# Expert stage of an encoder block on one core: eight pairs in a pipeline, rows gathered slot by slot, 16 KB weight rows, eleven weight halves loaded ahead

## What is computed

```python
def expert_choice_swiglu(h, w_router, w_gate, w_up, w_down):
    cap = EC_CAPACITY_FACTOR * seq // N_EXPERTS          # 64 slots per expert
    aff = softmax(einsum('bsd,de->bse', h, w_router))
    g, idx = lax.top_k(jnp.swapaxes(aff, 1, 2), cap)     # per expert, over tokens
    xin = h[idx]
    a = jnp.einsum('becd,edf->becf', xin, w_gate)
    u = jnp.einsum('becd,edf->becf', xin, w_up)
    y = jnp.einsum('becf,efd->becd', jax.nn.silu(a) * u, w_down) * g[..., None]
    return zeros.at[idx].add(y)                          # scatter-add of the rows

x = x + expert_choice_swiglu(rms_norm(x, norm2_g), ...)
return rms_norm(x, normf_g)
```

## Time and profile before

| | us |
|---|---|
| median of 3 runs | 959.29 (955.30 to 961.52) |
| the profiled execution, its own time | 957.11 |
| its span in the profile | 955.3 |
| PE busy | 884.0 (93%) |
| DVE, ACT, POOL busy | 340.6, 253.8, 22.8 |
| DMA | 239.66 MB, 251 GB/s over the span |

### The profile page before, as it was taken

The page is one execution under the profiler, slowest core; times in us unless marked ns, Lnnn a source line. Parts: engine busy times, 40 slices in busy tenths (PEclk is TensorE's granted clock), DMA queues, the critical chain, the costliest instruction groups (busy, mean ns, idle before and its releaser), DMA issues.

```text
span 955.3 us, 12190 instructions
## 1 busy us (share of the span) xinstructions
PE 884.0 (93%) x4932; PEld 573.9 (60%) x4932; DVE 340.6 (36%) x579; ACT 253.8 (27%) x488; POOL 22.8 (2%) x41
## 2 busy tenths in 40 slices
PE   4999899799989999997899988999899999899995
PEld 4999666577868888997635335353353533544432
DVE  4468767756625344337110032100230102301025
ACT  4433767665633323131111010110100100101102
POOL 1040000000000000000000000000000000000002
PEclk8999999999999999997999999999989999899997
DMA  8433111302137442916399999999999999999953
GB/s 258 94 90 89 45 45 45 110 17 83 39 112 241 138 121 61 372 53 264 133 378 409 410 409 384 381 409 410 408 410 405 410 410 409 410 409 410 410 236 110
DMA packets 115754, 239.66 MB, mean 251 GB/s; under 512 B 8960, under 2 KB 64384, under 8 KB 115456
## 3 DMA queue, kind: packets, MB, share of 16 engines
q1 hardware_dynamic: 110416, 235.95, 65.6%
q10 hardware_dynamic: 5296, 3.13, 1.2%
HBM read 236.96 MB, written 2.10 MB: 250 GB/s over the span
## 4 chain that ended last, share of the span: by engine, by line
PE 86%; DVE 7%; ACT 3%; issue 2%; DMA 1%; POOL 1%; SPq 0%; DVEq 0%; POOLq 0%; ACTq 0%
PE psum L1155 23%; PE psum L1186 12%; PE psum L819 10%; PE psum L821 10%; PE psum L820 10%; PE psum L1126 7%; PE psum L1203 3%; PE psum L956 2%; DVE x L1586 2%; PE psum L968 2%; DMA w_raw<-in_w_in 1%; PE psum L942 1%; PE psum L926 1%; PE psum L1169 1%; PE psum L978 1%
## 5 line engine op out<-in xcount | busy, mean ns | idle before, releaser
L1155 PE MATMUL psum<-wslot,xinT 128*64 128x512 f32 x1024 | 222.4, 593 | 4.9 <-ACT xinT L755 4.9
L1155 PEld LDWEIGHTS psum<-wslot,xinT 128*64 128x64 f32 x1024 | 72.5, 137 | 145.6 <-issue 139.3
L1186 PE MATMUL psum<-wslot,actT 128*64 128x512 f32 x512 | 111.6, 594 | 5.7 <-ACT actT L770 5.7
L1279 DVE TENSOR_TENSOR w_lo<-w_raw,w_hi 128x1024 fp32r<-128x1024 f32 (+1 forms) x56 | 65.2, 1185 | 77.3 <-ACT w_hi L543 77.0
L819 PE MATMUL psum<-hT_hi,w_hi 128*128 128x512 f32 x224 | 88.9, 397 | 1.4 <-DVE qB_next L1377 1.4
L821 PE MATMUL psum<-hT_hi,w_lo 128*128 128x512 f32 x224 | 87.5, 390 | 0.0
L820 PE MATMUL psum<-hT_lo,w_hi 128*128 128x512 f32 x224 | 87.4, 390 | 0.0
L1566 DVE TENSOR_TENSOR act<-act,psum 128x512 f32<-128x512 f32 x16 | 11.0, 688 | 210.5 <-ACT act L766 210.5
L1186 PEld LDWEIGHTS psum<-wslot,actT 128*64 128x64 f32 x512 | 36.5, 137 | 75.7 <-issue 71.1
L1126 PEld LDWEIGHTS psum<-pick,xn 128*128 128x128 f32 x512 | 62.8, 205 | 13.3 <-issue 6.5
L1126 PE MATMUL psum<-pick,xn 128*128 128x128 f32 x512 | 65.1, 290 | 5.4 <-DVE pick L1559 5.4
(11 more groups left out here) (169 smaller groups left out, 1181.0 us busy)
## 6 DMA issues: line engine op xcount, KB each, us to landing
wslot<-in_w_gate SPq DMA_DIRECT2D x64, 1024.0 KB, 14.1
wslot<-in_w_up SPq DMA_DIRECT2D x64, 1024.0 KB, 16.9
wslot<-in_w_down SPq DMA_DIRECT2D x64, 1024.0 KB, 10.8
w_raw<-in_w_in SPq DMA_DIRECT2D x40, 512.0 KB, 4.5
w_raw<-in_w_out SPq DMA_DIRECT2D x8, 512.0 KB, 7.5
x_in<-in_x SPq DMA_DIRECT2D x4, 512.0 KB, 10.4
w_raw<-in_w_o_a SPq DMA_DIRECT2D x8, 256.0 KB, 2.7
x<-in_x SPq DMA_DIRECT2D x1, 2048.0 KB, 7.8
```

The costliest lines, as they stand in the source:

```text
L1155: mm = pe.matmul(bank[4 * (i % 2) + n][CAP * f:CAP * f + CAP, :], xinT[:, HALF * h + k, CAP * (i % 2):CAP * (i % 2) + CAP], wslot[slot][:, ...
L1186: mm = pe.matmul(bank[(3, 5)[f]][CAP * e:CAP * e + CAP, :], actT[:, e, k, CAP * h:CAP * h + CAP], wslot[slot[e]][:, k, SEQ * f:SEQ * f + SEQ],
L1279: dve.tensor_tensor(lo, raw, hi.bitcast(F32), ALU.subtract).then_inc(w_split, 1)
```

## The change

1. **Loads.** A half is one DMA of 2 MiB. The rows of a matrix are dealt to the partitions differently (`(h p k) n` instead of `(h k p) n`), so that each partition reads four neighbouring rows, 16 KB in one piece. One semaphore per half: PE waits for whole halves. Nine buffers in turn and two that are used once (halves 5 and 7); eleven halves are loaded before the first is read, of which 5, 7, 9 and 10 are issued at `proj_done`, half 8 before it.
2. **Gather.** For a pair, the one-hot is the stationary operand and x2 (from pair 1 on a copy of x2, `x_gath`, that ACT makes during pair 0) the moving one: 4 matmuls of 128x512 per half of the features. The result has a slot per partition; ACT copies it out with the slot's 1/rms (`read_xin`), PE turns it by four transposes (`turn_xin`), DVE copies it with the gain (`read_turned_xin`). The slots' affinities and 1/rms are gathered for each pair (`gather_slots`, 8 small matmuls). `xn` and its four DVE passes go.
3. **Order.** No hardware loop: eight pairs written out. The gather of pair p+1, its transposes and the turned one-hot come between `gate_up` and `down` of pair p; the scatter of pair p-1 is laid piece by piece after every weight row group (two matmuls) of `gate_up` of pair p. The last pair's scatter stands alone as before.
4. **Route stage.** More clock-keeping transposes: 14 before the affinities are turned, 18 after, 12 instead of 9 after each of the eight rounds, 8 after the last, 5 and 6 more around the first transposes of the gathered rows.

```diff
-SLOTS = 8
+SLOTS = 9
+AHEAD = 11
...
-    xn = sb("xn", [NT, D], 32)
+    x_gath = sb("x_gath", [NT, D], W0 + 64)
...
+        ONCE = {5: SLOTS, 7: SLOTS + 1}
+        recurring = [m for m in range(len(HALVES) * PAIRS) if m not in ONCE]
...
-                rows = matrix[0, 4 * q + 2 * pr + e].rearrange("(h k p) n -> h p k n", h=4, p=P)[2 * h + part]
-                sp.dma_start(wslot[slot][:, QUARTER * part:QUARTER * (part + 1), :], rows)\
-                    .then_inc(w_slot_in[slot][part], 16)
+                rows = matrix[0, 2 * p + e].rearrange("(h p k) n -> h p (k n)", h=2, p=P)[h]
+                slot = slot_of(m)[0]
+                sp.dma_start(wslot[slot][:, :, :].rearrange("p k n -> p (k n)"), rows)\
+                    .then_inc(w_slot_in[slot], 16)
...
+            for m in (5, 7, 9, 10):
+                load_half(m)
+            for m in range(AHEAD, len(HALVES) * PAIRS):
+                wait_half_used(sp, recurring[recurring.index(m) - SLOTS])
+                load_half(m)
...
+            keep_clock(14)
             pe.wait_ge(aff_done, NT)
...
+            keep_clock(18)
             for n in range(CAP // 8):
                 pe.wait_ge(eight_taken, n + 1)
-                keep_clock(9)
+                keep_clock(12)
+            keep_clock(8)
...
+            def gather_slots(p, into):
...
+                for c in range(NT):
+                    pe.matmul(into[:, 0:2], pick[:, c, :, :], aff[:, c, 2 * p:2 * p + 2],
+                              start=(c == 0), stop=(c == NT - 1))
+                for c in range(NT):
+                    mm = pe.matmul(into[:, 2:3], pick[:, c, :, :], rstd[:, c:c + 1],
+                                   start=(c == 0), stop=(c == NT - 1))
...
+                for c in range(NT):
+                    mm = pe.matmul(bank[6 + f][:, :], pick[:, c, :, :], (x_gath if p else x2)[:, c, cols],
+                                   start=(c == 0), stop=(c == NT - 1))
...
+                for k in range(HALF):
+                    t = pe.transpose(bank[6 + f][:, P * k:P * k + P], rows[:, k, :], ident[:, :])
...
+                            if between is not None:
+                                between(2 * HALF * h + HALF * n + k)
...
+                def scatter_before(step):
+                    if 3 <= step < 11:
+                        scatter(p - 1, step - 3)
...
+                gate_up(p, 0, scatter_before if p else first_between)
+                gate_up(p, 1)
+                if p + 1 < PAIRS:
+                    gather_slots(p + 1, bank[1])
+                    gather(p + 1, 0)
+                turn_act(2 * p)
+                if p + 1 < PAIRS:
+                    gather(p + 1, 1)
+                    turn_xin(p + 1, 0)
+                turn_act(2 * p + 1)
+                if p + 1 < PAIRS:
+                    turn_xin(p + 1, 1)
+                    turn_pick(p + 1, bank[3])
+                down(p)
```

More of the change, by code:

```diff
@@ L238, in encoder_block @@
         m_lo_done = sem("m_lo_done")
-        w_slot_in = [[sem(f"w_slot{i}_{part}_in") for part in ("first", "second")] for i in range(SLOTS + 1)]
-        w_slot_used = [sem(f"w_slot_used{i}") for i in range(SLOTS + 1)]
+        w_slot_in = [sem(f"w_slot_in{i}") for i in range(AHEAD)]
+        w_slot_used = [sem(f"w_slot_used{i}") for i in range(AHEAD)]
         router_in = sem("router_in")
@@ new lines, in high_y @@
+            def high_y(p):
+                wait_half_used(act_, half_at(p, w_down, 1, 1))
+                act_.wait_ge(slot_aff_done, 2 * p + 2)
+                if p:
+                    act_.wait_ge(added, 8 * p)
+                for f in range(2):
+                    act_.activation(y_hi[:, SEQ * f:SEQ * f + SEQ], bank[4 + f][:, :], ACT.Copy,
+                                    scale=slot_aff[:, p % 2:p % 2 + 1]).then_inc(y_hi_done, 1)
+            read_xin(0, 0)
+            read_xin(0, 1)
@@ L1193, in scatter @@
-                def scatter(pr):
-                    pe.wait_ge(give_done, 2 * q + 2)
-                    for n in range(8):
-                        f, c = divmod(n, NT)
-                        if c == 0:
-                            pe.wait_ge(y_lo_done, 4 * q + (2 * pr + f + 1))
-                        pe.wait_ge(added, 16 * q + (8 * pr + max(n - 1, 0) + 1))
-                        for part in (y_hi, y_lo):
-                            mm = pe.matmul(bank[6 + n % 2][:, :], give[:, pr, P * c:P * c + P],
-                                           part[:, SEQ * f:SEQ * f + SEQ], start=(part is y_hi),
-                                           stop=(part is y_lo))
-                        mm.then_inc(scattered, 1)
@@ L1208, in experts @@
-                gather(0, 0)
-                pe.wait_ge(pick_done, 2 * q + 2)
-                if not first:
-                    pe.wait_ge(actT_done, 4 * q)
-                for pr in range(2):
-                    for c in range(NT):
-                        mm = pe.matmul(bank[2][:, 2 * pr:2 * pr + 2], pick[:, c, 2 * pr:2 * pr + 2, :],
-                                       aff[:, c, bass.ds(4 * q + 2 * pr, 2)], start=(c == 0), stop=(c == NT - 1))
-                mm.then_inc(slot_aff_turned, 1)
@@ L1232, in experts @@
[L1232 to L1248 removed]
+                            if k == HALF - 1:
+                                mm.then_inc(w_slot_used[slot], 1)
@@ new lines, in scatter @@
+            def scatter(p, n):
+                f, c = divmod(n, NT)
+                if n == 0:
+                    pe.wait_ge(give_done, p + 1)
+                if c == 0:
+                    pe.wait_ge(y_lo_done, 2 * p + f + 1)
+                if n < 2 and p + 1 < PAIRS:
+                    pe.wait_ge(xin_done, 2 * (p + 1) + n + 1)
+                elif n >= 2 or p:
+                    pe.wait_ge(added, 8 * p + n - 1)
+                for part in (y_hi, y_lo):
+                    mm = pe.matmul(bank[6 + n % 2][:, :], give[:, p % 2, P * c:P * c + P],
+                                   part[:, SEQ * f:SEQ * f + SEQ], start=(part is y_hi), stop=(part is y_lo))
+                mm.then_inc(scattered, 1)
@@ L1251, in _ @@
+            for n in range(8):
+                scatter(PAIRS - 1, n)
         @block.vector
@@ L1596, in experts @@
[L1596 to L1609 removed]
+                    dve.tensor_copy(slot_aff[rows, p % 2:p % 2 + 1], src[rows, e:e + 1]).then_inc(slot_aff_done, 1)
```

476 lines of the change are left out of this document (227 added, 249 removed).

## The result

The changed kernel takes 950.61 us (median of 20 runs, 948.41 to 955.98) against 960.92 us for the kernel before in the same sessions (20 runs). The ratio is 0.9907, 95% interval 0.9891 to 0.9923: just under 1% faster, 3.6 us above the forecast of 947 and inside its range. The profiled execution has a span of 948.0 us, against 955.3 before. Single executions of both kernels fall in two groups (of the kernel before, 4 of the 20 lie at 955 to 957 us and 16 at 959 to 963; of the changed kernel, 10 at 948 to 950 and 10 at 951 to 956), and a ratio moves a little with how many of each it holds.

The account below looks back on a forecast made before the run. PE was taken as the bound, with the weights' DMA close behind. Start 465.0 plus pairs 462.3 gave 927.3 us; with the 18.4 tail a span of 945.7, with 1.8 around it 947.5, forecast as 947; range 932 to 958.

Parts of the forecast that it names:

- The pair: PE's time for one pair of experts after the change: 59.1 us, against 61.1 before.
- gather's pass of 0.43: Each 512-column matmul pass of the new gather takes PE 0.43 us; 16 passes make 6.9 us a pair.
- A scatter piece: Each lone scatter piece within gate and up costs PE 0.80 us with its switches, 6.4 us a pair.
- The rival in which the switches are partly hidden: Scatter pieces in gate and up cost only 0.50 us each, a pair 56.7; time 932 (with 410 GB/s: 949); chance 0.22.
- Pairs 0 and 7: First and last pair of the expert stage on PE: 57.9 us and 49.8 us.
- The start: Chain from pick to the first gate and up: it begins at 465.0 us, against 464.8 before.
- so they delay nothing at the full clock: Route stage: 136 filling transposes take PE 15 us, against the 15.45 us that DVE takes, so no delay.
- they don't: Transposes don't hold the clock: they take 29 us, the expert stage starts some 13 us late; time 960; chance 0.03.
- rest of 14 us: In pair 0 the weight DMA rests some 14 us, near 502 to 516, whatever its speed.
- The last half: Last weight half, at 428 GB/s with 16 KB rows, is in at 904.6 us, 16 us before PE wants it.
- 4 KB pieces: Weight rows stay in 4 KB pieces or HBM binds: last half in at 922, time 949 us; chance 0.10.
- The tail: From the end of the last down to the end, final scatter and norm: 18.4 us, unchanged.

Follow-up runs that it names:

- the twos: Changed kernel with two scatter pieces after every second weight row group instead of one after every one: 941.92 us, ratio 0.9837 to the kernel before.
- the block's run: Changed kernel with all eight scatter pieces of a pair in one block after the third step of gate and up: 948.37 us, ratio 0.9899.
- the old clock keeping: Changed kernel without the added clock-keeping transposes, 9 after each round as in the kernel before: 953.69 us, ratio 0.9918.
- the run in one pass: Changed kernel with the slots' affinities and 1/rms gathered by 4 matmuls of 3 columns a pair, not 4 of 2 and 4 of 1: 942.22 us, ratio 0.9814.

## Why the prediction was right, and where it was off

**The pair.** Predicted 59.1, measured 59.15. The gather's pass of 0.43 is right (3.54 and 3.44 for 8). Slots take 1.87 with their switches, predicted 1.9. A scatter piece costs 0.66 and the two passes of gate behind it 1.01 where a stream has 0.86: 0.82 in all, against the 0.80 read from the attention's timeline. That the switch costs this much is shown from the other side by the twos, 0.35 for each one saved. The rival in which the switches are partly hidden, 0.50 a piece, falls by that. Term by term the sum holds: gate and up 27.4 (said 27.5), down 13.9 (13.75), gather 7.0 (6.9), slots 1.87 (1.9), 20 transposes with their switches 2.4 (2.7), scatter 6.5 (6.4); the misses, 0.3 on the transposes and 0.1 each on the others, cancel.

**Pairs 0 and 7.** 58.2 and 50.2, predicted 57.9 and 49.8. The terms named for pair 0 make 57.1 (59.1 - 6.4 for the scatter + 3.5 for half a gather + 0.9 for eight transposes), so 0.8 of the 57.9 stands there without a term; measured, the half gather and the transposes take 5.6 us with the breaks that they make in gate and up (58.2 - 59.15 + 6.5), where the terms have 4.4.

**The start.** Predicted 465.0, measured 466.0. The step that failed is "so they delay nothing at the full clock": the 14 transposes were counted among the filling under DVE's 15.45 us, but they stand ahead of the affinities' turn, for which DVE waits. From the end of the router logits to DVE's first round it is 437.31 to 441.02, 3.71 us, where before it was 438.07 to 440.52, 2.45; here is the row of the kernel before from which that is counted:

```profile
434.57 3.50 PE psum L1075 x32
```

That is 1.3 us, and the run without the 14 gives the same. The chain from slots to first gate took 7.8 where 7.5 was said, and the 0.2 taken off for a turn at the full clock is already spent in the 1.3. Against these 1.8 stand 0.8 that are no part of the change: the router logits ended that much sooner in this profile. Their end lies at 435.9 to 437.3 in four profiles of the changed order and at 440.0 to 441.0 in the seven others, so I compare starts from that line on. The two groups go with the clock: in the four it is granted at 1.00 from 24 us to there, in the seven it falls once on the way, at about 180 us (0.69 from 178 to 182 in the run without the 14, where the changed kernel has 1.00) or, in the block's run, at about 100.

**The clock.** In the profile of the changed kernel it is 0.96 in 440 to 450 and 1.00 in 450 to 460, where the old clock keeping has 0.55 and 0.96 and drops to 0.69 in 460 to 470. The rival "they don't", a stage 13 us late, did not come true. But in one profile of ten with added transposes the clock did fall, at 464, for 1.9 us of delay; so they mostly hold it, and not surely. The statement of the Trainium skill (TensorE: Matmul & The Clock Gate, Part 4) that the full clock does not engage for transposes is not borne out: in the kernel before it rose from 0.50 in 440 to 445 to 1.00 in 449 to 450 under nothing but transposes. Whether they alone hold it is left open by the fall at 464. What they are worth at the start, by single profiles, is 3.0 us between the end of the router logits and the first gate (30.4 without any, 27.4 without the 14), of which the 14 give back 1.3; in the measured time it is a wash.

The clock in the stage itself the prediction left out. It built the new pair from the full clock, rightly, but it took the old 61.1 us a pair for PE's work and waits, and named only waits as what would go. Some 5 us of the old 472.1 were work at 0.50 at two turns of the quads, shown above. The time came out right all the same, as the sum doesn't use the old pair; the account of the gain was incomplete.

**The weights.** The rest of 14 us is there, from 505 to 518. The rate in the middle is 427, predicted 428. The last half was to land at 904.6 and landed at about 911. The stream starts again at 518.3, not 517.5, takes until about 522 to come to its rate (279 GB/s in 519 to 520, 377 and 344 in the next two), and from 520 to 904 its mean is 425, with slices of 416 to 422 between those of 429 in the strip: 3 us more for 79 halves. The term was sized from a 3 us stretch of x2's load and missed these dips. (The packet times that stand beside it there, 4 x 0.15 to 0.16 us against 0.61, don't carry the 5% by themselves: they give anything from nothing to 5%. The rates do.) It had no effect, as PE wanted that half at 922.4. The rule in the Trainium skill (DMA: Bandwidth & Descriptors, section Bandwidth) that the HBM side binds at about 358 GB/s does not hold here: 409 with 4 KB rows, 427 with 16 KB rows. The prediction read it too strictly, for the same section gives about 358 as what each core gets when both cores of an HBM domain stream, and 425 as measured for 16 MB with the pair's other core idle; this program runs on one core, and its 427 is near that. On the length of the row the rule says nothing. But the size of the case "4 KB pieces" was too mild in the prediction: it said 949, 2 us over the forecast. The run shows 7 us over the changed kernel (0.9985 against 0.9907), because the last half landed at 931.4 and not at 922. Of these 9 us the later start of that profile is some 4 (its stream starts again at 521 to 522) and the slow start after the rest is 2; the remainder, 2 to 3, I have not traced.

**The tail.** 18.4 taken over, 18.6 measured. The sum of the spans came out 2.3 high: 1.0 from the start, 1.1 in the eight pairs (0.3 in pair 0, 0.4 in pair 7, 0.05 in each of the others), 0.2 in the tail. The rest of the 3.6 lies between the profiled execution (948.0 and 1.8 around it) and the median.

**Why so large a rewrite moved the time so little.** From the first gate to the end of down it takes 463.4 us where it was 472.1, 1.1 us a pair over all eight. PE's waits fell from 25.1 to 0.9 us there, and the 5 us of work at the low clock went with them; so, as an estimate from these numbers, some 20 us came back as new PE work and switches: slots gathered every pair in two passes (0.89 of it needless, as the run in one pass shows), 8 interruptions where 4 would do (1.4 a pair), 14 transposes on the path (1.3). Undoing these alone wins another 1.4%, and there the weights stop it. No run takes the new gather or the new order by itself out or puts it into the kernel before, so the share of each is read from the traces alone, and that PE's standing at the turns of the quads is what brought the clock down is argued, not tested.

## What to carry to other kernels

When an engine is busy nine tenths, count what an edit adds to it in switches between kinds of work, and not in instructions alone: laying pieces singly between others hides a wait and buys a switch for each; grouping them in twos, which two banks and DVE kept up with, had the best of both (threes and fours were not tried). When compute and transfers are within a few per cent of each other, an edit of one shows its worth only together with the other; here PE's gain without the long rows moved next to nothing, and in the kernel before, whose PE never waited for weights in this stage, the long rows alone had nothing to win (that they bring nothing there was not tried). Filling that keeps a clock up belongs behind the instruction on which the next engine waits; ahead of it, it cost 0.9 to 1.4 us here. And look at the granted clock of the kernel before at each turn of its stage: what seems the price of a wait can be the wait and, behind it, work at half the clock.

## What I had not expected of the hardware

- 4.4% more transfer rate from row length, at equal bytes and with the halves in the same order: 409 GB/s with 4 KB rows and 427 with 16 KB over 700 to 800 us, both with a DMA share of 1.01 to 1.03.
- An interruption of the 64-column float32 stream by fp32r matmuls costs 0.35 to 0.36 us there and back beyond the work itself, for one piece (0.66 + 1.01 - 0.86 - 0.46) as for two (1.13 + 1.87 - 1.72 - 0.92).
- The end of the same router logits, in kernels whose instructions up to there are the same, came at 435.93, 437.31, 440.24 and 440.96 in four profiles, a spread of 5.0 us, more than any edit of the start was worth. The late ones have a fall of the granted clock long before, at about 100 or 180 us, which the early ones lack.
- PE busy without a break at 1.00 for 17 us, with transposes and the small matmuls of the slots, did not keep the clock in one profile (0.50 from 464 to 467); under the same instructions it stayed at 1.00 in the profile of the changed kernel.
